# Decoder step on one core: jobs of the first attention at other steps, and the token factor of two norms moved behind the up products

## The reference, cut to what matters

```python
def rms_norm(x, g):
    y = xf * lax.rsqrt(jnp.mean(xf * xf, axis=-1, keepdims=True) + EPS)
    return (y * g)
def conv_ffn(hn, conv_state, w_up, conv_w, conv_b, w_down):
    u = hn @ w_up
    uc = jnp.concatenate([conv_state, u], axis=1)
    c = sum((conv_w[j] * uc[:, j:j + T] for j in range(CONV_W)), conv_b)
    gate, val = jnp.split(c, 2, axis=-1)
    return (jax.nn.silu(gate) * val) @ w_down, uc[:, T:]
...
h = h + mix
f, ncs = conv_ffn(rms_norm(h, ffn_norm_g[layer]), cs, ...)
h = h + f
```

## Time and profile before

| | |
|---|---|
| median of three runs | 2937.64 us (2934.67 to 2940.99) |
| the profiled execution | 2938.89 us |
| its span, first to last instruction | 2937.1 us |
| PE busy | 2698.7 us, 92% of the span |
| DVE busy | 1733.6 us, 59% |
| ACT busy | 980.9 us, 33% |
| POOL busy | 740.7 us, 25% |
| mean granted TensorE clock | 0.949 of full |

### The profile page before, as it was taken

The page is one execution under the profiler, slowest core; times in us unless marked ns, Lnnn a source line. Parts: engine busy times, 40 slices in busy tenths (PEclk is TensorE's granted clock), DMA queues, the critical chain, the costliest instruction groups (busy, mean ns, idle before and its releaser), DMA issues.

```text
span 2937.1 us, 45747 instructions
## 1 busy us (share of the span) xinstructions
PE 2698.7 (92%) x17524; PEld 2627.8 (89%) x17524; DVE 1733.6 (59%) x2724; ACT 980.9 (33%) x1818; POOL 740.7 (25%) x362
## 2 busy tenths in 40 slices
PE   4999999778887999999999969698979999999997
PEld 3999999677776999999999958598979999999997
DVE  6787831555545565556555676795266555556555
ACT  3666632665303212121211245584132211112120
POOL 2111113344304222222222142173232222222220
PEclk7999999888788999999999989898999999999998
DMA  3322243434344343443444111444613545434331
GB/s 104 92 72 86 73 127 103 137 110 124 104 144 94 83 90 83 90 83 94 97 91 94 37 39 58 130 144 127 138 40 88 103 92 92 91 83 87 93 76 61
DMA packets 219857, 275.65 MB, mean 94 GB/s; under 512 B 29562, under 2 KB 191746, under 8 KB 217666
## 3 DMA queue, kind: packets, MB, share of 16 engines
q1 hardware_dynamic: 219746, 274.17, 37.4%
HBM read 237.90 MB, written 125.62 MB: 124 GB/s over the span
## 4 chain that ended last, share of the span: by engine, by line
PE 82%; DVE 7%; DMA 3%; POOL 2%; ACT 2%; issue 2%; SPq 1%; DVEq 0%; POOLq 0%; ACTq 0%
PE acc L347 23%; PE acc L349 23%; PE acc L348 23%; DVE arena L579 2%; PE aux L1971 2%; PE aux L1566 1%; PE acc L1491 1%; PE acc L1958 1%; PE acc L1534 1%; DVE arena L555 1%; POOL xl L533 1%; PE acc L1941 1%; PE aux L636 1%; PE aux L635 1%; PE acc L1525 1%
## 5 line engine op out<-in xcount | busy, mean ns | idle before, releaser
L347 PE MATMUL acc<-xh,w_hi 128*128 128x344 f32 x3504 | 1135.8, 324 | 65.6 <-DVE xl L533 37.0
L349 PE MATMUL acc<-xh,w_lo 128*128 128x344 f32 x3504 | 1126.5, 321 | 0.0
L348 PE MATMUL acc<-xl,w_hi 128*128 128x344 f32 x3504 | 1126.2, 321 | 0.0
L332 POOL TENSOR_TENSOR w_lo<-w_raw,w_hi 128x1024 fp32r<-128x1024 f32 x194 | 485.7, 2508 | 1761.9 <-ACT w_hi L322 1761.9
L347 PEld LDWEIGHTS acc<-xh,w_hi 128*128 128x128 f32 x3504 | 664.6, 190 | 85.1 <-issue 39.2
L349 PEld LDWEIGHTS acc<-xh,w_lo 128*128 128x128 f32 x3504 | 664.9, 190 | 0.0
L348 PEld LDWEIGHTS acc<-xl,w_hi 128*128 128x128 f32 x3504 | 664.8, 190 | 0.0
L852 DVE TENSOR_TENSOR hT<-hT,acc 128x1032 f32<-128x1032 f32 x184 | 226.3, 1230 | 387.8 <-PE acc L349 387.8
L322 ACT CAST w_hi<-w_raw 128x1024 fp32r<-128x1024 f32 x194 | 201.8, 1050 | 582.9 <-PE acc L349 495.4
L347 PE MATMUL acc<-f_hi,w_hi 128*128 128x344 f32 x1056 | 340.2, 322 | 11.1 <-DVE f_lo L1111 11.1
L349 PE MATMUL acc<-f_hi,w_lo 128*128 128x344 f32 x1056 | 339.5, 322 | 0.0
(11 more groups left out here) (261 smaller groups left out, 3202.5 us busy)
## 6 DMA issues: line engine op xcount, KB each, us to landing
out_a_w_sample<-in_cache_a_kv_w SPq DMA_DIRECT2D x23, 2848.0 KB
w_raw<-in_ffn_w_up SPq DMA_DIRECT2D x88, 512.0 KB, 3.8
scratch<-arena SPq DMA_DIRECT2D x46, 516.0 KB, 3.1
w_raw<-in_ffn_w_down SPq DMA_DIRECT2D x44, 512.0 KB, 3.5
w_raw<-in_a_w_in SPq DMA_DIRECT2D x36, 512.0 KB, 4.3
out_a_w_sample<-in_cache_a_kv_w SPq DMA_DIRECT2D x8, 2044.0 KB
arena<-in_cache_a_kv_w SPq DMA_DIRECT2D x24, 512.0 KB, 3.8
w_raw<-scratch SPq DMA_DIRECT2D x17, 512.0 KB, 3.9
```

Source lines behind the costliest of these rows:

```text
L332: pool.tensor_tensor(w_lo[:, slot, :], w_raw[:, slot, :], w_hi[:, slot, :].bitcast(F32), ALU.subtract).then_inc(lo_ready, 1)
L347: pe.matmul(out, whi, ahi, start=first, stop=False)
L348: pe.matmul(out, whi, alo, start=False, stop=False)
L349: return pe.matmul(out, wlo, ahi, start=False, stop=last)
```

## The change

Two parts, which share no instruction.

**Norms 1 and 4.** `xh` is now ACT's copy of `hT` scaled by the gain alone, `xl` DVE's `hT * g − xh`; neither needs the factor, so both start while the output projection is still running, and POOL has no part in them. The matmul of the squares stands inside the first up product, ahead of its seventh chunk, in the other set of accumulators. The factor is multiplied into every `u` instead (4 x 11 per layer), as a first step of `conv_dve`, with a semaphore of its own.

**First attention.** The value jobs of groups 1 and 2 come two steps earlier, and their loads are issued in the step of the job before; the first key job of a pair comes two steps later; the shares of the weights come one to two steps later and stand at other places of ACT's list, `weights_pool` stands behind the splits of its step; weighing, mixing and the cast of the mixed output come two steps later. The sum is made in the buffer of group 2, and group 0's outputs of odd pairs are kept in `a_mix`.

The diff, cut to its core:

```diff
-            for j in range(KC):
-                wait_normed(pe, n, j)
+            for e, j in enumerate(split_rows(n)):
+                wait_normed(pe, n, e)
+                if e == STAT_AT and n in LATE:
+                    norm_pe(pe, n)
...
+        LATE, STAT_AT = (1, 4), 6
...
+            return [4, 5, 6, 7, 0, 1, 2, 3] if n == 1 else range(KC)
...
+            act.activation(xh[:, k, :], hT[:, k, :], ACT.Copy, scale=norm_g[:, n, k:k + 1]).then_inc(n_hi, 1)
...
+            v.wait_ge(n_hi, 8 * n + e + 1)
+            v.scalar_tensor_tensor(xl[:, k, :], hT[:, k, :], norm_g[:, n, k:k + 1], xh[:, k, :].bitcast(F32),
+                                   ALU.mult, ALU.subtract).then_inc((n_lo, n_lo_odd)[e % 2], 1)
...
         def bout_dve(v):
...
-            square_dve(v, 4, KC - 1)
+            for e in range(KC):
+                split_lo_dve(v, 4, e)
+                if e == 3:
+                    square_dve(v, 4, KC - 1)
...
         def ffn_pe(pe, l):
-            norm_pe(pe, 1 + 3 * l)
...
             mm.then_inc(w_used, 1)
+            pe.wait_ge(n_stat, 2 * STAT[1 + 3 * l] + 1)
             turns(pe, l, ffn_turn_pe)
...
         def conv_dve(v, l, n, which, ch, s, products):
...
             v.wait_ge(f_raw, products)
+            v.tensor_tensor(u[:, 2:U1], u[:, 2:U1], rinv[:], ALU.mult).then_inc(u_scaled, 1)
+            v.wait_ge(u_scaled, n + 1)
             v.tensor_scalar(c[:, 0:T], u[:, 2:U1], w[2], w[3], ALU.mult, ALU.add).then_inc(conv_step, 1)
...
-        K_JOBS = ((-7, 0, 7, 1), (-2, 1, 4, 4), (2, 2, 0, 4), (4, 2, 4, 4))
+        K_JOBS = ((-5, 0, 7, 1), (-2, 1, 4, 4), (2, 2, 0, 4), (4, 2, 4, 4))
...
+        def weighed(i, g):
+
+            return a_mix if g == 0 and i % 2 else a_og[g]
...
+        def values_at(k):
+
+            return [x for x in range(A_GRP) if k == first_a(x) + (1, -1, -1)[x % NG]]
+
+        def after(k, steps):
+
+            return [i for i in range(A_PAIRS) if k == 10 * (i + 1) + steps]
...
         def o_evac(eng, copy, x, half, done):
...
-            if i:
-                wait_emptied(eng, ("w", i - 1, g, 1))
+            o = weighed(i, g)
+            if g == 0:
+                if i >= 2:
+                    eng.wait_ge(DA.mixed, 4 * (i - 2) + 2)
+            elif i:
+                eng.wait_ge(DA.mixed, 4 * i)
+                if g == 2:
+                    eng.wait_ge(DA.o_lo, 2 * i)
...
         def attn_a_act(act):
...
-                if 0 <= i < A_PAIRS and r == 4:
-                    sums_act(act, i)
+                for i in after(k, 5):
+                    shares_act(act, i)
                 if 0 <= k - 2 < A_UNITS:
                     probs_a(act, act.copy, k - 2, 0, DA.out_act)
                 if 0 <= k < A_UNITS:
                     exps_a_act(act, k, 1)
-                if 0 <= i < A_PAIRS and r == 3:
-                    shares_act(act, i)
+                for i in after(k, 6):
+                    sums_act(act, i)
...
-                if 0 <= i < A_PAIRS and r == 9:
+                for i in after(k, 11):
                     mixed_act(act, i, 0)
                     mixed_act(act, i, 1)
...
+        def mix_pool(pool, i, g):
...
+                pool.tensor_tensor(a_og[g][:, cols], a_og[g][:, cols], weighed(i, g - 1)[:, cols], ALU.add) \
+                    .then_inc(DA.mixed, 1)
...
         def attn_a_pool(pool):
             for k in range(-AHEAD, A_STEPS):
-                i, r = divmod(k - 10, 10)
-                if 0 <= i < A_PAIRS and r == 3:
+                for i in after(k, 5):
                     shares_pool(pool, i)
-                if 0 <= i < A_PAIRS and r == 4:
+                for i in after(k, 6):
                     sums_pool(pool, i)
-                if 0 <= i < A_PAIRS and r == 5:
-                    weights_pool(pool, i)
                 for x in splitting(k):
                     split_a_lo(pool, x, "k")
                 for x in splitting(k - 1):
                     split_a_lo(pool, x, "q")
...
+                for i in after(k, 7):
+                    weights_pool(pool, i)
+                for g in (1, 2):
+                    for i in after(k, 8 + g):
+                        mix_pool(pool, i, g)
+                for i in after(k, 11):
+                    mixed_pool(pool, i)
```

More of the change, by code:

```diff
@@ L559, in norm_act @@
                 act.wait_ge(n_mm, STAT[n] + 1)
-                act.activation(thirds(rinv[:]), acc_set(0), ACT.Ln, bias=eps[:], scale=1.0 / D).then_inc(n_stat, 1)
+                act.activation(thirds(rinv[:]), acc_set(n in LATE), ACT.Ln, bias=eps[:], scale=1.0 / D).then_inc(n_stat, 1)
                 act.wait_ge(n_stat, 2 * STAT[n] + 1)
                 act.activation(rinv[:], rinv[:], ACT.Exp, scale=-0.5).then_inc(n_stat, 1)
-            for k in range(KC):
-                act.wait_ge(n_x, 8 * n + k + 1)
+            for k in range(KC if n not in LATE else 0):
+                act.wait_ge(n_x, 8 * NX[n] + k + 1)
                 act.copy(xh[:, k, :], xf_n[k % XF]).then_inc(n_hi, 1)
@@ L902, in aout_dve @@
                     square_dve(v, 1, n - 1)
-            square_dve(v, 1, KC - 1)
+                if n >= 6:
+                    split_lo_dve(v, 1, n - 6)
+            for e in range(2, KC):
+                split_lo_dve(v, 1, e)
+                if e == 5:
+                    square_dve(v, 1, KC - 1)
         def bout_pe(pe):
@@ L1291, in jobs_at @@
             names = []
-            for x in starting(k - 1):
+            for x in values_at(k):
                 names += [("v", x, 0), ("v", x, 1)]
             names += [("k", n) for n in key_jobs_at(k)]
-            i, r = divmod(k - 10, 10)
-            if 0 <= i < A_PAIRS:
-                names += [("stat", i)] if r == 1 else []
-                names += [("w", i, r - 6, half) for half in range(2)] if 6 <= r < 9 else []
+            names += [("stat", i) for i in after(k, 1)]
+            names += [("w", i, g, half) for g in range(NG) for i in after(k, 8 + g) for half in range(2)]
             if 38 <= k < 38 + NG:
@@ L1454, in attn_a_sp @@
                         .then_inc(DA.k_out[stage], 16)
-                i, r = divmod(k - 10, 10)
-                if 0 <= i < A_PAIRS and r == 2:
+                for i in after(k, 2):
                     wait_emptied(sp, ("stat", i))
@@ L1595, in attn_a_pe @@
                     key_rows_pe(pe, n)
-                i, r = divmod(k - 10, 10)
-                if 0 <= i < A_PAIRS and r == 1:
+                for i in after(k, 1):
                     stats_pe(pe, i)
-                if 0 <= i < A_PAIRS and 6 <= r < 9:
-                    weights_pe(pe, i, r - 6)
+                for g in range(NG):
+                    for i in after(k, 8 + g):
+                        weights_pe(pe, i, g)
                 if 38 <= k < 38 + NG:
@@ L1749, in attn_a_dve @@
                     key_rows_dve(v_, n)
-                i, r = divmod(k - 10, 10)
-                if 0 <= i < A_PAIRS and 6 <= r < 9:
-                    weigh_dve(v_, i, r - 6)
+                for g in range(NG):
+                    for i in after(k, 8 + g):
+                        weigh_dve(v_, i, g)
                 if 38 <= k < 38 + NG:
@@ L1758, in attn_a_dve @@
                     probs_a(v_, v_.tensor_copy, k - 2, 1, DA.out_dve)
-                if 0 <= i < A_PAIRS and r == 3:
+                for i in after(k, 4):
                     shares_dve(v_, i)
```

114 lines of the change are left out of this document (60 added, 54 removed).

## The result

The changed kernel takes 2949.32 us (median of 11 runs, 2944.69 to 2954.62) against 2940.85 for the one before (11 runs). The ratio is 1.0029, 95% interval 1.002 to 1.0039: slower by 8.5 us, where 2926 and "faster" were forecast. The time lies inside the whole range, 2898 to 2950; the sign is wrong. The profiled execution has a span of 2947.4 us, 10.3 above that of before.

The account below looks back on a forecast made before the run. PE was taken to bound the kernel (82% of the chain). Norms −30, multiply +24.6 and attention −6 gave −11.4 against 2938.89: 2927.5, or 2926 as median (execution 1.25 above it); own range 2914 to 2938, whole range 2898 to 2950.

Parts of the forecast that it names:

- Norms: Norms 1 and 4: earlier split and statistics inside the up product shorten PE's waits; −30 us, between −19 and −41.
- Multiply: FFN convolutions: of a turn's four multiplies only the second half's value delays PE; +24.6 us, between 0 and +35.
- rival B: FFN: the multiply is hidden, as the block of 2.07 that L1095 suffers goes; 2902 us, chance 0.12.
- Attention: First attention: removed waits of 34.4 and added stops of 34.7 cancel, the clock gains; −6 us, between −40 and +35.
- c': First attention: `weights_pool` behind its step's split, which waits for ACT's cast, stops PE's weights some 4.7 us, in two periods.
- (a): First attention: `mix_pool` behind POOL's rest of the next key holds group 1's output evacuation, up to 5.4 us.
- (b): First attention: query's rest, two mixes or rests and `mixed_act` before group 2's output evacuation hold ACT; 5.8 us.
- What remains is the clock ... I take all, 6: First attention: with waits cancelling, matmuls of periods one and two run at period three's rate, saving 3.3 and 3.0 us.
- I count all as gone: First attention: PE's waits for value loads (14.6), key stage (13.3) and ACT's copy (6.5) all vanish; 34.4 us.
- Rival D: First attention: POOL's late mix holds ACT, and only 14.6 of 34.4 go; +20 without clock gain, 2952 us, chance 0.20.
- Rival C: First attention: the 34.4 go, additions hide in POOL's and ACT's idle time; −34 instead of −6, 2898 us, chance 0.18.

Follow-up runs that it names:

- norms_psum: Kernel before with the norm part alone, the FFN multiply on the path done by DVE while taking the product out of PSUM; ratio 0.9892 to the kernel before.
- no_multiply: Changed kernel without the multiply by the token factor in all 88 convolutions; ratio 0.9958 to the kernel before.
- attn_only: Kernel before with the attention part of the change alone; ratio 1.007 to the kernel before, +21 us.
- pool_order: Changed kernel with POOL's last weights step, the mixing, and the mixed output's rest and cast ahead of the splits; ratio 0.9881 to the kernel before.
- best: Changed kernel with weights and mixing ahead of the splits, and the path's multiply done by DVE out of PSUM; 2883.89 us, ratio 0.9812 to the kernel before.
- jobs_only: Kernel before with the earlier value jobs, their loads and the later first key job alone; ratio 1.0004 to the kernel before.
- late_only: Changed kernel with weights and mixing ahead of the splits, value jobs, their loads and first key job at their old steps; ratio 0.9933 to the kernel before.
- norms_only: Kernel before with the norm part of the change alone, multiply in the convolutions included; ratio 0.997 to the kernel before, −9 us.
- mix_first: Changed kernel with POOL's mixing and the mixed output's rest and cast ahead of the splits; ratio 0.9935 to the kernel before.

## Why the prediction was wrong

**Norms: right.** −30 forecast, −32.7 in the trace, −33 by `norms_psum`. The evacuation was forecast 19.7 us behind the last add and came at 20.2; the prediction had Ln and Exp beside the product, but with what follows them on ACT they held the evacuation.

**Multiply: right.** +24.6 forecast, +22.5 in the trace. POOL took the place forecast for it, and rival B's lost block did not vanish but moved from the second tap to the first. The Trainium skill's rule on the shared port (page "SBUF — State Buffer", section "SBUF: two separate sides") agrees with the trace: whoever starts first holds it for a whole instruction, and the first tap, 0.82 alone, took 2.62 beside POOL's 2.50. The shift was 1.15, not 1.25 to 1.43, and by `no_multiply` the other three convolutions were covered.

**Attention: wrong, and with it the sign.** −6 forecast, +18.6 measured in the pair of traces, and +21 us by `attn_only`. The new stops were named in the right places and at nearly the right length: c' 4.7 forecast, 5.03 and 5.04 measured; (a) 5.4, ACT held 5.45; (b) 5.8, ACT held 4.51 (how 4.7 and 5.8 are made up, the prediction doesn't say). Of the stops to be removed the value loads' went, and the key stage's but for 2.1; at ACT's copies PE waits 8.7 where it waited 6.5, now behind the mix's rest. And old and new did about cancel: PE's idle time rose by 5.8. The step that failed is "What remains is the clock ... I take all, 6": the clock did not give back 6 but took 12.7, as the same matmuls were busy for 254.3 us instead of 241.6 at granted 0.81 instead of 0.83 (11.3 on the means of the traces of both attentions). I argued that the new stops were shorter than the old. They were not: 8.61 with 3.83 behind it, 5.04, then 7.38 with 4.40, in stretches at granted 0.78 and 0.80. Per stop, the weights' 5.03 delayed the units by 7.2 and the mix's 8.61 + 3.83 by 16.1: 1.4 us of delay per us of stop on the mean of the four, counted against the kernel before. Taken out together, 27 us of idle time were worth 45.4 us in `pool_order` and 38.4 in `best`, 1.7 and 1.4. That a stop lowers the clock behind it is read from the granted clock and the busy times; what the clock answers to stays open, and busy time doesn't follow idle time in each row of the table (`jobs_only`, `late_only`).

A second step holds only in part: "I count all as gone". The copies' wait stayed, as said, and `jobs_only` shows that without the later shares and sums the jobs take away the value loads' wait and little else, which is then worth nothing that shows. The later shares and mix, in the good order, are worth 19 us at `aout` without the jobs (`late_only`).

Rival D had the sign and the size (+20 without a clock gain; measured 18.6 to 21), through the mix's hand-over as it said. Its condition was not met, though: less than 23 of the 34.4 had to go, and 25.8 went (14.6 and 11.2), even with none of the copies' counted. It had 20 us more of idle time; there were 5.8, and slower matmuls made up the sum. So its size is in part luck. Rival C comes near to what the attention does once POOL's order is mended: −27 at `aout` in `pool_order` (799.73 to 772.88) and −20 in `best`, of C's −34. (B's 2926 − 24.6 is 2901, not 2902, which changes nothing.)

The stretch behind the attention, +2.7, has no instruction of the change; its matmuls were busy 84.2 instead of 81.5 us at granted 0.79 instead of 0.82. It is not the changed attention's price: in `no_multiply`, with the same attention, the stretch took 90.4 us as in the kernel before.

## What to carry to other kernels

An in-order list on a helper engine is read for what stands *behind an instruction that waits*: three short operations that others needed at once stood behind splits that nobody needed for several steps, and moving them ahead turned a loss into the largest gain of the case. Removing a wait can be worth nothing while other waits on the same path stay (`jobs_only`); try each move alone and with the others. And where a stage runs below full clock, a PE stop can cost more than its length (here 1.4 to 1.7 times), so waits that cancel in length need not cancel in time. Time in such a stage is read from more than one execution.

## What had not been expected of the hardware

Matmuls of the stretch behind the attention, from the first product of `aout` to its first chunk that waits for the sample tokens, ran at very different clocks in kernels that don't differ there. In thirteen traces this stretch takes one of three lengths, always with 8.8 or 8.9 us of idle time: 90.4 us at granted 0.82 (before, `norms_only`, `norms_psum`, `no_multiply`), 93.1 at 0.79 (seven kernels, the changed one among them) or 110.6 at 0.65 (`mix_first`, `late_only`). `mix_first`:

```profile
794.90:905.53 110.63, 101.78 (x473) 93.00 (x473) 33.73 (x59) 6.63 (x12) 7.05 (x3) 0.65 0.38 120
```

The 17.6 us above the changed kernel's 93.1 are most of the reason why that execution has a span of 2944.5 where the kernel's median is 2925.08 (2917.5 to 2946.3). What picks one of the three, the traces don't show.
